# Values of the last sample: weighted and summed on TensorE in column groups, heads kept with a mask on VectorE

## What is computed

```python
def block_attend(q, k_rows, v_rows, valid):
    s = jnp.einsum('bhqd,bhqrd->bhqr', q, k_rows).astype(F32) * (ATT_HEAD_DIM ** -0.5)
    p = jax.nn.softmax(jnp.where(valid, s, NEG_SCORE), axis=-1)
    return jnp.einsum('bhqr,bhqrd->bhqd', p.astype(v_rows.dtype), v_rows)
...
    ya = (ya * jax.nn.silu(az)) @ w_att
    ym = (ym * jax.nn.silu(mz)) @ w_mlstm
    u = jax.nn.sigmoid(ga) * ya + jax.nn.sigmoid(gm) * ym
    y = x + gate[:, None] * (u @ w_out)
```

## Time and profile before

| what | us |
|---|---|
| median of 3 runs | 756.62 (756.18 to 757.75) |
| profiled execution, its time | 757.0 |
| its span, first to last instruction | 755.3 |
| TensorE matmul busy | 688.0 (91%) |
| VectorE busy | 482.8 (64%) |
| GpSimd busy | 464.3 (61%) |
| ScalarE busy | 338.2 (45%) |
| mean granted TensorE clock | 0.949 |

### The profile page before, as it was taken

The page is one execution under the profiler, slowest core; times in us unless marked ns, Lnnn a source line. Parts: engine busy times, 40 slices in busy tenths (PEclk is TensorE's granted clock), DMA queues, the critical chain, the costliest instruction groups (busy, mean ns, idle before and its releaser), DMA issues.

```text
span 755.3 us, 14932 instructions
## 1 busy us (share of the span) xinstructions
PE 688.0 (91%) x5066; PEld 618.9 (82%) x5066; DVE 482.8 (64%) x468; ACT 338.2 (45%) x760; POOL 464.3 (61%) x293
## 2 busy tenths in 40 slices
PE   2899999998988889999999999995899999999992
PEld 0576888786867858988999999985889998999992
DVE  0530589898988975895696597667665369343222
ACT  5634474646353335454463563530422225233554
POOL 4211266685756515898789679666594656666651
PEclk9898899999989979999999999999699999999996
DMA  8976858988788761277866768659247365832102
GB/s 315 336 253 220 243 174 249 272 252 271 237 269 265 215 207 29 87 237 208 250 199 185 216 208 241 182 177 240 56 122 212 97 181 154 266 85 83 57 0 113
DMA packets 156904, 144.71 MB, mean 192 GB/s; under 512 B 7547, under 2 KB 115152, under 8 KB 156852
## 3 DMA queue, kind: packets, MB, share of 16 engines
q1 hardware_dynamic: 142696, 136.10, 60.0%
q10 hardware_dynamic: 14164, 8.07, 3.4%
HBM read 135.10 MB, written 9.11 MB: 191 GB/s over the span
## 4 chain that ended last, share of the span: by engine, by line
PE 33%; issue 23%; POOL 20%; DVE 11%; SPq 6%; DMA 4%; ACT 1%; POOLq 0%; DVEq 0%; ACTq 0%
PE ps L545 26%; POOL sb_wL L1417 8%; POOL sb_arenaA L1491 8%; POOL sb_arenaA L1459 3%; DMA sb_arenaA<-in_w_ada 3%; DVE sb_arenaA L1728 2%; SPq L392 2%; SPq L393 2%; DVE sb_arenaA L1870 1%; PE ps L579 1%; DVE sb_arenaA L1875 1%; DVE sb_arenaB L1875 1%; DVE sb_arenaA L1732 1%; PE ps L653 1%; PE ps L900 1%
## 5 line engine op out<-in xcount | busy, mean ns | idle before, releaser
L1417 POOL TENSOR_TENSOR sb_wL<-sb_wraw,sb_wH 128x512 fp32r<-128x512 f32 (+1 forms) x176 | 236.3, 1359 | 200.0 <-ACT sb_wH L960 183.7
L545 PE MATMUL ps<-sb_hH,sb_wH 128*128 128x260 f32 x1152 | 241.6, 292 | 1.6 <-ACT sb_arenaB L965 0.9
L545 PE MATMUL ps<-sb_hL,sb_wH 128*128 128x260 f32 x1152 | 235.5, 287 | 0.0
L545 PE MATMUL ps<-sb_hH,sb_wL 128*128 128x260 f32 x1152 | 235.1, 286 | 0.0
L545 PEld LDWEIGHTS ps<-sb_hH,sb_wH 128*128 128x128 f32 x1152 | 181.7, 193 | 14.9 <-issue 10.6
L960 ACT ACTIVATE sb_wH<-sb_wraw 128x512 fp32r<-128x512 f32 (+1 forms) x176 | 104.1, 613 | 195.0 <-PE ps L545 158.6
L545 PEld LDWEIGHTS ps<-sb_hL,sb_wH 128*128 128x128 f32 x1152 | 181.6, 193 | 0.0
L545 PEld LDWEIGHTS ps<-sb_hH,sb_wL 128*128 128x128 f32 x1152 | 181.2, 192 | 0.0
L1491 POOL TENSOR_TENSOR sb_arenaA<-sb_arenaA 128x2048 f32<-128x2048 f32 x32 | 116.0, 3631 | 5.0 <-DMA sb_arenaA<-in_cache_v 3.0
L1732 DVE TENSOR_REDUCE sb_arenaA<-sb_arenaA 128x2048 f32 (+1 forms) x32 | 72.9, 2284 | 4.4 <-DVE sb_arenaA L1728 2.5
L1459 POOL TENSOR_TENSOR sb_arenaA<-sb_arenaA 128x2048 f32<-128x2048 f32 x11 | 54.3, 4939 | 29.5 <-DMA sb_arenaA<-in_cache_k 29.5
(11 more groups left out here) (356 smaller groups left out, 949.9 us busy)
## 6 DMA issues: line engine op xcount, KB each, us to landing
sb_wraw<-in_w_in SPq DMA_DIRECT2D x64, 512.0 KB, 5.2
sb_arenaA<-in_cache_k SPq DMA_DIRECT2D x128, 256.0 KB, 3.1
sb_arenaA<-in_cache_v SPq DMA_DIRECT2D x128, 256.0 KB, 3.3
sb_arenaA<-in_w_ada SPq DMA_DIRECT2D x6, 2048.0 KB, 12.4
sb_arenaB<-in_state_C SPq DMA_DIRECT2D x8, 512.0 KB, 3.9
sb_wraw<-in_w_mlstm SPq DMA_DIRECT2D x8, 512.0 KB, 4.4
sb_wraw<-in_w_out SPq DMA_DIRECT2D x8, 512.0 KB, 3.7
sb_arenaB<-in_x_prompt SPq DMA_DIRECT2D x1, 2048.0 KB
```

Source lines behind the costliest of these rows:

```text
L545: last = mm(ps[:, 2 * s + a, 0:HALF], w[:, s, k, :], x[:, k, a * HALF:(a + 1) * HALF], start=(k == 0 and w is wH and x is xH), stop=(k == ...
L1417: tt(wL[:, j % 2, part], wraw[:, j % 4, part], wH[:, j % 2, part].bitcast(F32), ALU.subtract)\
```

## The change

For the last sample (steps 4 to 7 of pass 3) GpSimd no longer multiplies and VectorE no longer sums over pages. TensorE takes the weights in `score` as its stationary operand, 32 columns (4 pages x 8 heads) of a step, and the page as its moving operand, one matmul per page. Page g of a step goes to PSUM partitions 32g to 32g + 31 of bank 6, and the four steps add up there. A partition holds the sum over positions for one page's place and one head's weights, over all eight heads' values; of the 32 rows of a group only eight belong to the page itself, and in each of these only the 64 columns of its own head. `own_head` is a mask that is 1 at partition 40g + h, column h. VectorE multiplies bank 6 by it into vacc[1] and gives the eighth vsum_rdy, and page_sums goes on as before, into bank 7. GpSimd's last mLSTM pass is written out of its loop, without the two steps, and GpSimd waits for the values before its loop, since that writes over `score`.

```diff
+        own_head = sb("own_head", [P, AH])
...
+            def last_values(s):
+
+                pe.wait_ge(ld_page[s % 4], 64 * (8 + 2 * (MH - 1) + s // 4 + 1))
+                at = (8 * (MH - 1) + s) * 32
+                for g in range(STEP_PAGES):
+                    last = mm(ps[32 * g:32 * g + 32, 6, :], score[:, at:at + 32], page[:, s % 4, g * AW:(g + 1) * AW],
+                              start=(s == 4), stop=(s == 7))
+                return last
+
+            for s in (4, 5):
+                last_values(s)
             ztile(3, T_GATE + 3, hH, hL)
-            page_sums(MH, 6, 0).then_inc(ys_mm, 1)
+            for s in (6, 7):
+                last = last_values(s)
+            last.then_inc(sam_pe, 1)
             pe.wait_ge(abc_rdy, 1)
+            page_sums(MH, 7, P).then_inc(ys_mm, 1)
...
-            sums_leave(MH, 6, 0).then_inc(ys_ev, 1)
+            sums_leave(MH, 7, P).then_inc(ys_ev, 1)
...
+            chain(nc.gpsimd.memset(own_head[:, :], 0.0))
+            for g in range(4):
+                chain(nc.gpsimd.affine_select(out=own_head[:, :], in_=own_head[:, :], compare_op=ALU.not_equal, fill=1.0,
+                                              base=-40 * g, pattern=[[-1, AH]], channel_multiplier=1))
...
-            with pool.Fori(0, MH - 1) as i:
-                h = i + 1
+            def mlstm(h, last):
...
                     if j == 5:
                         value_step(7, h - 1)
-                    else:
+                    elif j < 10 or not last:
                         value_step(j - 6, h)
-            value_step(6, MH - 1)
-            value_step(7, MH - 1)
+
+            with pool.Fori(0, MH - 2) as i:
+                mlstm(i + 1, False)
+            mlstm(MH - 1, True)
...
             decayed_state(0, 0)
+            pool.wait_ge(sam_pe, 4)
...
-            value_pair(4, MH - 1, False)
             dve.wait_ge(sam_pe, 1)
...
-            value_pair(6, MH - 1, False)
-
             chain(tt(goS[:, :, :], goS[:, :, :], over(vcol[:, V_MG:V_MG + KT], B), ALU.mult))
             tt(goS[:, :, :], goS[:, :, :], gzS[:, :, :], ALU.mult)
+            dve.wait_ge(sam_pe, 4)
+            tt(vacc[1].rearrange("p (h n) -> p h n", h=AH), ps[:, 6, :].rearrange("p (h n) -> p h n", h=AH),
+               over(own_head[:, :], DH), ALU.mult).then_inc(vsum_rdy, 1)
```

More of the change, by code:

```diff
@@ L2018, in _ @@
             chain.end(3)
-            dve.wait_ge(sam_pe, 4)
+            dve.wait_ge(sam_pe, 5)
             v.tensor_copy(rbc[:, :, :].rearrange("p b n -> p (b n)"), ps[:, 7, 64:96]).then_inc(sam_dve, 1)
```

## The result

| what | before | changed |
|---|---|---|
| median of 20 runs each, in turn | 754.05 us (750.6 to 759.23) | 750.14 us (744.46 to 754.47) |
| profiled execution, its time | 757.0 | 748.81 |
| its span | 755.3 | 747.1 |
| abc broadcast to ztile(2) of the loop | 47.41 | 42.05 |
| ztile(2) to the end of the span | 202.7 | 204.2 |

The ratio is 0.9942, 95% interval 0.9918 to 0.9965: 4.4 us faster (2.6 to 6.2), where 5.3 was forecast; the two medians are 3.9 apart. The three runs of before that the prediction started from lay in the upper part of this kernel's own spread; its median of 20 is 2.6 lower.

A forecast was written before the change was run, and what follows sets the result against it. The kernel's time was taken to move with V through the second strand. V came 5.3 us earlier after 3.84 of values and 0.69 of mask, so 756.6 - 5.3 = 751.3, range 749.8 to 754.2.

The forecast's parts named there:

- V: Moment vsum_rdy reaches 8, at 530.06 before; forecast at 524.7, 5.3 us earlier.
- The values' price, 3.84: Sixteen matmuls added on TensorE ahead of V, 1.92 on each side of gate tile 3.
- Rivals 2 and 5: Column groups overlap less (753.3, chance 0.05), or run one behind another, 13.8 in place of 3.84 (761.3, chance 0.06).
- Mask, copies, sums_leave: Around V: VectorE's masked product takes 0.69; behind ScalarE's copies sums_leave starts at V + 3.7, key_query at V + 4.5.
- The second strand: VectorE, ScalarE and GpSimd work from V to the loop's ztile(2), V + 22.6; forecast to move by 5.3, to 547.3.
- From there to the end the same length: From the loop's ztile(2) to the span's end: 202.7 as before, or up to 2 more with a low clock.
- rival 1: Clock falls at TensorE's new wait before the loop's ztile(2), 1.7 lost; result 753.0, chance 0.19.
- Faster: Whole kernel: time below 755.1, chance 0.87.
- Rival 3: All of TensorE's hole before ztile(2) goes, not held by the second strand: 9.0 earlier, 747.6, chance 0.07.
- 4 (V moves alone): GpSimd's decayed state or low(2) is held by a load of its own; time stays 756.6, chance 0.07.
- The pages: Step 7's last pages land by some 517 and are wanted at 523: no cost, 6 us of cover.
- GpSimd's longer start and its unrolled pass: Five more first instructions, some 2 us, fall into 14.24 of idle time; the written-out last mLSTM pass gains nothing.

The follow-up runs named there:

- e_sums: Changed kernel with VectorE's two long sums back, over the same pages with unused results, ahead of the mask; 750.49 us, ratio 0.994.
- e_none: Changed kernel with only one page's matmul left of eight on each side of the tile; 745.44 us, ratio 0.985.
- e_serial: Changed kernel with all sixteen values matmuls in one column group, adding onto each other; 758.64 us, ratio 1.0055.
- e_full_before_2: Second run of the e_full_before kernel; 745.63 us, ratio 0.9902 to the kernel before.
- e_full_before: Kernel before, reordered: gate tile 4 ahead of page sums, tile 6's high and low parts early, yaL late; 746.54 us, ratio 0.9876.
- e_hoist_before: Kernel before with low(2) and its high part put ahead of yaH and yaL; 755.03 us, ratio 0.9997.

## Why the prediction was right or wrong, point by point

- **What bounds the kernel.** Right. V and its strands decide: V moved by 5.32 against the abc broadcast, and ztile(2) by 5.36; e_sums, e_none and e_serial moved V by 1.98, -1.76 and 10.24, and the stretch by 1.99, -1.76 and 10.28.
- **The values' price, 3.84.** Right: 1.92 on each side, from the row of another kernel part with the same form. The four groups overlap with weights from `score`, too. Rivals 2 and 5 fall, with a factor of 3.67 by e_serial. The Trainium skill, TensorE: Matmul & The Clock Gate, section Measured speedup vs the span model, has 2.38 for three column tiles; here, with four tiles, the measured factor is higher, and decides.
- **Mask, copies, sums_leave.** The mask took 0.69 as the earlier trace rows had it. sums_leave stood 3.56 behind V, not 3.7, and key_query 4.1 behind V, not 4.5, and the page sums ran at the full clock (1.92 in place of 3.58, 520.53 to 522.45); that time was hidden.
- **The second strand takes over.** Right: TensorE waited for it, 2.11. Forecast was 3.7, or some 1 (0.7 by its own sum) if the earlier gap brought a low clock. It did bring one: the two tiles with their key_query took 15.1 (524.52 to 539.60), not 13.2, nor the 16.2 of before.
- **"From there to the end the same length", 202.7. This is the step that failed.** It measured 204.2. The forecast took the wait at ztile(2) as free, so that its sum has nothing for the clock behind it, and gave the clock's fall behind it (rival 1) 0.19. It fell in five of five profiles with such a wait, at a cost of 1.5 where rival 1 had 1.7. The prediction had the row for it, and argued it away in two ways: that 0.69 of idle time had cost nothing, which says nothing on 2 to 4 us, and that a fall in the earlier gap would shorten the wait to about 1. The fall in the earlier gap came, but the wait was still 2.11, and the clock fell again behind it.
- **The sum.** Against its own kernel: -5.36 + 1.5 = -3.85 by the marks, -4.4 (2.6 to 6.2) timed; forecast was -5.3. The starting point, 756.62, was 2.6 too high as the median of three runs. From 754.05 with rival 1's terms, -5.3 + 1.7, one has 750.4; 750.14 was measured. The range of 749.8 to 754.2 held the time, near its lower end, but by luck: it was the sum of two errors of opposite sign, a start 2.6 too high and 1.5 of clock left out.
- **Chances.** "Faster" at 0.87 came true by the ratio; the line of 755.1 itself says nothing, as the unchanged kernel's median of 20 lies below it, at 754.05. Rival 3 (all of the hole goes) and 4 (V moves alone) are excluded by the strand's rows.
- **The pages.** Right: in e_sums the sum that waits for the last two could begin 12.45 after the abc broadcast, and in the changed kernel steps 6 and 7 begin 16.85 after it.
- **GpSimd's longer start and its unrolled pass:** the abc broadcast, to which they would show, stands at 500.85 and 502.03, within the 499.80 to 505.20 of before. A gain or loss under 3 us from them could not be seen.

## What to carry to other kernels

When a change lengthens a wait ahead of a long dense stretch of TensorE, as from 0.7 to 2.1 us here, put a fall of the clock behind it into the sum and do not leave it to a rival (1.5 us here, in five of five profiles); matmuls of no use in the gap gave that back in the one profile of them. Ask what TensorE could do while the others work: here the order of the next tiles was worth more (-7 by the marks) than the change (-4), and the two together most (-13). Size a term by marks inside the profile and take the starting time from many runs, since a median of three was off by as much as half of the effect.

## What the runs showed of the hardware

- Four column groups of 32 with f32 operands: eight matmuls 128*32 x 128x512 in 1.92 us, 7.05 when they run in one group.
- The clock fell behind waits of 1.68 to 2.17 before ztile(2) in five of five profiles, behind a wait of 1.74 in two of fourteen at another place, and behind a wait of 0.87 in two of fourteen at a third. Those behind ztile(2) lasted some 3.4 us each and made the rest about 1.5 longer; the two behind the 1.74 cost 1.2 and 1.3.
- Behind a wait of 2.58 it fell as well (e_full_before_2, 0.83 over 518 to 520 and 0.50 over the next 2 us), but not behind 0.69 or 0.76 before ztile(2), nor behind 1.02 (e_full_before).
- Behind the same idle time the low clock need not come at the same moment: with 10.07 and 10.08 of idle time before the page sums it began some 5.0 after the idle time did in the profile of before and some 2.2 after in that of e_hoist_before, and it ended 7.6 and 4.8 after key_query began.
